# Both feed-forward layers of a decoder trunk by seven block products in place of eight

## The reference, cut to what matters

```python
D_MODEL = 1024; SEQ = 1024; DEPTH = 2; FFN_HIDDEN = 2816      # all float32

def swiglu(h, w_gate, w_up, w_down):
    return (jax.nn.silu(h @ w_gate) * (h @ w_up)) @ w_down

for layer in range(DEPTH):
    h = rmsnorm(x, mix_norm_w[layer])
    x = x + (attn_pool_mixer(h, ...) if layer % 2 == 0 else ssd_mixer(h, ...))
    h = rmsnorm(x, ffn_norm_w[layer])
    x = x + swiglu(h, w_gate[layer], w_up[layer], w_down[layer])
return rmsnorm(x, final_norm_w)
```

## Time and profile before

| what | value |
|---|---|
| median of three runs | 2565.6 us (2565.22 to 2565.96) |
| span of the profiled execution | 2561.2 us |
| PE busy, weight loads busy | 98%, 80% of the span |
| DVE, ACT, POOL busy | 39%, 31%, 25% |
| DMA traffic, mean | 54 GB/s |
| feed-forward of layer 0 | from 326.7 to 1055.2 us |
| feed-forward of layer 1 | from 1834.1 to the end |

### The profile page before, as it was taken

How to read it: one execution, slowest core, us unless ns; L and a number is a source line. 1 busy time by engine, 2 the same in 40 slices (tenths; PEclk the granted TensorE clock), 3 DMA queues, 4 the chain that set the end, 5 groups by cost and what they waited for, 6 DMA issues and landing times.

```text
span 2561.2 us, 30302 instructions
## 1 busy us (share of the span) xinstructions
PE 2507.6 (98%) x11642; PEld 2038.2 (80%) x11642; DVE 1001.9 (39%) x1474; ACT 803.2 (31%) x1311; POOL 627.6 (25%) x340
## 2 busy tenths in 40 slices
PE   7999999999999999999999999999999999999998
PEld 5866788888888888777887887887888888888887
DVE  5345432222222222648438348448522222222224
ACT  4044421111111111448238247248411111111112
POOL 2222222222222222124214214324222222222220
PEclk9999999999999999999999999999999999999999
DMA  4110111111111111112112112212111111111111
GB/s 146 50 33 1 41 60 48 43 46 44 49 49 49 49 49 49 36 58 91 37 59 88 51 49 83 58 51 82 50 58 49 49 49 49 49 49 49 49 33 66
DMA packets 167848, 137.54 MB, mean 54 GB/s; under 512 B 14160, under 2 KB 152284, under 8 KB 167772
## 3 DMA queue, kind: packets, MB, share of 16 engines
q1 hardware_dynamic: 164444, 128.85, 16.7%
q10 hardware_dynamic: 3328, 7.60, 0.8%
HBM read 132.11 MB, written 4.33 MB: 53 GB/s over the span
## 4 chain that ended last, share of the span: by engine, by line
PE 91%; DVE 4%; issue 2%; ACT 2%; POOL 0%; DMA 0%; DVEq 0%; ACTq 0%; POOLq 0%
PE ps L840 28%; PE ps L842 28%; PE ps L841 28%; PE ps L1012 1%; PE ps L980 1%; PE ps L1179 1%; PE ps L873 1%; DVE acc L1514 1%; PE ps L1166 1%; DVE mdec L1553 1%; PE ps L1004 1%; DVE yx L1582 1%; PE ps L1171 1%; DVE xres L1269 1%; DVE xn_lo L1299 1%
## 5 line engine op out<-in xcount | busy, mean ns | idle before, releaser
L840 PE MATMUL ps<-xn_hi,w_hi 128*128 128x512 f32 x2208 | 865.9, 392 | 7.9 <-DVE xn_lo L1299 4.8
L841 PE MATMUL ps<-xn_lo,w_hi 128*128 128x512 f32 x2208 | 860.6, 390 | 0.0
L842 PE MATMUL ps<-xn_hi,w_lo 128*128 128x512 f32 x2208 | 860.1, 390 | 0.0
L474 POOL TENSOR_TENSOR w_lo<-w_raw,w_hi 128x1024 fp32r<-128x1024 f32 x206 | 497.5, 2427 | 1453.8 <-ACT w_hi L564 1453.5
L840 PEld LDWEIGHTS ps<-xn_hi,w_hi 128*128 128x128 f32 x2208 | 415.1, 188 | 100.5 <-issue 12.6
L842 PEld LDWEIGHTS ps<-xn_hi,w_lo 128*128 128x128 f32 x2208 | 415.1, 188 | 87.1
L841 PEld LDWEIGHTS ps<-xn_lo,w_hi 128*128 128x128 f32 x2208 | 415.3, 188 | 84.9
L564 ACT ACTIVATE w_hi<-w_raw 128x1024 fp32r<-128x1024 f32 x206 | 212.5, 1053 | 541.6 <-PE ps L842 357.4
L1434 DVE TENSOR_TENSOR hid<-ps,gate 128x512 f32<-128x512 f32 x88 | 60.9, 692 | 802.4 <-ACT gate L668 802.4
L1269 DVE TENSOR_TENSOR xres<-ps,xres 128x512 f32<-128x512 f32 x368 | 251.2, 690 | 203.8 <-PE ps L842 203.8
L668 ACT ACTIVATE gate<-ps 128x512 f32<-128x512 f32 x88 | 52.6, 598 | 747.0 <-PE ps L842 747.0
(11 more groups left out here) (189 smaller groups left out, 2148.7 us busy)
## 6 DMA issues: line engine op xcount, KB each, us to landing
w_raw<-in_w_gate SPq DMA_DIRECT2D x44, 512.0 KB, 3.8
w_raw<-in_w_up SPq DMA_DIRECT2D x44, 512.0 KB, 4.0
w_raw<-in_w_down SPq DMA_DIRECT2D x44, 512.0 KB, 3.4
w_raw<-in_ssd_w_in SPq DMA_DIRECT2D x40, 512.0 KB, 3.9
mdec<-decay_sums SPq DMA_DIRECT2D x32, 512.0 KB, 3.6
w_raw<-in_ssd_w_out SPq DMA_DIRECT2D x16, 512.0 KB, 4.3
out<-xn ACTq DMA_DIRECT2D x8, 512.0 KB, 2.6
xres<-in_x SPq DMA_DIRECT2D x6, 512.0 KB, 8.4
```

Of the source, the lines that this page charges most:

```text
L474: pool.tensor_tensor(w_lo[piece.slot][:, :], raw[piece.raw][:, :], f(w_hi[piece.slot][:, :]), ALU.subtract).then_inc(lo_done, 1)
L840: pe.matmul(dst, l_hi, r_hi, start=first, stop=False)
L841: pe.matmul(dst, l_hi, r_lo, start=False, stop=False)
L842: return pe.matmul(dst, l_lo, r_hi, start=False, stop=last)
```

## The change

It splits tokens, model width and hidden width in two each, and makes a 2 x 2 by 2 x 2 block product from seven products of sums of blocks (Strassen's scheme in Winograd's form, M1 to M7) in place of eight.

- **Gate and up, stage one.** A pair is 256 hidden columns (`NP` = 11 pairs). A pair has seven products for gate and seven for up. A product is 4 blocks x 3 = 12 matmuls of 512 tokens. M3, M4, M6 and M7 are added by PE on top of a PSUM bank that already holds M5, M7, M1 and M6; before that ACT copies the bank out (`copy_out`). Of the weights, POOL makes four sums per matrix and pair (`w_sum`), ACT seven high parts (`p_hi_of`), POOL seven low parts (`p_lo_of`), each 128 x 512: POOL has 22 such instructions a pair. Gate and up share one set of buffers, so the sum of up can be made only when the same product of gate is done.
- **Token side, once a layer.** The input sums (`comb`, T1 to T4 of the blocks) are made from the last four token tiles as they are transposed: DVE `tail_t1` to `tail_lo2`, ACT `tail_first` to `tail_hi4`, POOL `tail_lo3`, `tail_sum4`, `tail_lo4`. They are written out between the work of pair 0.
- **Hidden layer.** ACT and DVE assemble the four blocks of gate and up, DVE multiplies and makes the sums S1 to S4, and SP stores seven blocks of 128 x 512 a pair to DRAM (`hidden`, 1.8 MB a pair).
- **Down, stage two.** 7 products x 11 pairs = 77 slices of 4 token tiles x 3 = 12 matmuls. SP loads a slice's hidden block and one to two weight blocks (256 KB each) into a ring of five; POOL makes one low part, ACT two high parts, DVE one low part, for 44 slices also a weight sum (`slice_sum`), and between them 56 adds to the residual (`add_down`).
- **Residual.** It is parked in DRAM (`parked_x`) during stage one, as its 32 KB a partition serve as work space, and is loaded again during slices 5 to 19.
- The norms after layer 0 and 1 are placed in the last product of stage two (`plain`, `final`) and behind it. The loops over rounds are written out.

The diff, cut:

```diff
+FIRST_PAIR = ("M1g", "M2g", "M1u", "M2u", "M5g", "M6g", "M3g", "M7g", "M5u", "M4g", "M6u", "M3u", "M7u")
+NEXT_PAIR = ("M2g", "M5g", "M6g", "M3g", "M7g", "M1u", "M4g", "M2u", "M5u", "M6u", "M3u", "M7u")
...
+        hidden = nc.dram_tensor("hidden", (NP, P, 7 * BANK), F32, kind="Internal").ap()
...
+        DOWN = ("M1", "M2", "M5", "M6", "M4", "M7", "M3")
+        ADDS_TO = {"M1": ((4, 0), (4, 1), (0, 0), (0, 1)), "M2": ((4, 0),), "M5": ((4, 1), (0, 1)),
+                   "M6": ((4, 1), (0, 0), (0, 1)), "M4": ((0, 0),), "M7": ((0, 0), (0, 1)), "M3": ((4, 1),)}
...
+                def store_hidden(p):
+                    sp.wait_ge(h_ready, h_order.count(layer, p, "S3"))
+                    sp.dma_start(hidden[p], h_set).then_inc(h_stored, 16)
...
+                sp.wait_ge(out_full, 2 * NT * (1 + layer * G))
+                load_wv("u", 0)
+                for p in range(NP):
+                    if p + 1 < NP:
+                        sp.wait_ge(p_lo_done, lo_order.count(layer, p, "M4g"))
+                        load_wv("g", p + 1)
+                    if p:
+                        store_hidden(p - 1)
+                    sp.wait_ge(p_lo_done, lo_order.count(layer, p, "M4u"))
+                    if p + 1 < NP:
+                        load_wv("u", p + 1)
...
+                def load_slice(j, p):
+                    s, n = j * NP + p, DOWN[j]
+                    i = s % RING
+                    if s in (2, 3):
+                        sp.wait_ge(product_full, product_order.count(layer, NP - 1, "M7u"))
...
+                    elif s >= RING:
+                        sp.wait_ge(down_full, down_count(layer, 0, s - RING))
...
+                    sp.dma_start(s_val[i][:, :], hidden[p][:, j * BANK:(j + 1) * BANK]).then_inc(ring_loaded[i], 16)
...
+                        load_d(d12[p], 0, 1)
+                        load_d(d_val[i][:, :], 0, 0)
...
+                for p in range(4):
+                    load_slice(0, p)
+                store_hidden(NP - 1)
+                back = [4, 0, 5, 1, 6, 2, 7, 3]
+                for s in range(4, SLICES):
+                    load_slice(s // NP, s % NP)
+                    if 5 <= s < 5 + 2 * NT and s % 2:
+                        tt = back[(s - 5) // 2]
+                        sp.wait_ge(parked[tt % 2], 16 * (layer * NT // 2 + tt // 2 + 1))
+                        if s == 5:
+                            sp.wait_ge(h_stored, 16 * (layer + 1) * NP)
...
+                    a, b, op = {5: (a21, a22, ALU.add), 6: (p_val[5][:, :, :], a11, ALU.subtract),
+                                3: (a12, p_val[6][:, :, :], ALU.subtract), 7: (a11, a21, ALU.subtract)}[n]
+                    pool.tensor_tensor(p_val[n][:, :, :], a, b, op).then_inc(sum_ready, 1)
...
+                p_lo_of(0, "M1g")
+                p_lo_of(0, "M2g")
+                tail_lo3(0)
+                tail_sum4(0)
+                w_sum(0, "g", 5)
+                w_sum(0, "g", 6)
+                p_lo_of(0, "M1u")
+                p_lo_of(0, "M5g")
+                p_lo_of(0, "M2u")
+                w_sum(0, "g", 3)
+                p_lo_of(0, "M6g")
+                p_lo_of(0, "M3g")
+                w_sum(0, "g", 7)
+                p_lo_of(0, "M7g")
+                for i in range(1, 4):
+                    tail_lo3(i)
+                tail_lo4(0)
+                for i in range(1, 4):
+                    tail_sum4(i)
+                    tail_lo4(i)
+                p_lo_of(0, "M4g")
+
+                def sums_and_lo(p, m):
+                    w_sum(p, m, 5)
+                    w_sum(p, m, 6)
+                    p_lo_of(p, "M5" + m)
+                    w_sum(p, m, 3)
+                    p_lo_of(p, "M6" + m)
+                    p_lo_of(p, "M3" + m)
+                    w_sum(p, m, 7)
+                    p_lo_of(p, "M7" + m)
+
...
+                for s in range(SLICES):
+                    pool.wait_ge(s_hi_done, layer * SLICES + s + 1)
+                    pool.tensor_tensor(s_lo[s % RING][:, :], s_val[s % RING][:, :], f(s_hi[s % RING][:, :]), ALU.subtract)\
+                        .then_inc(s_lo_done, 1)
...
+                    act.dma_start(parked_x[tt], xres[:, tt, :]).then_inc(parked[tt % 2], 16)
+                    square(tt, ffn_xn(tt))
...
+                copy_out(0, "M1g")
+                tail_hi2(1)
+                tail_hi3(1)
+                tail_hi2(2)
+                tail_hi3(2)
+                p_hi_of(0, "M6g")
+                tail_hi2(3)
+                tail_hi3(3)
+                p_hi_of(0, "M3g")
+                p_hi_of(0, "M7g")
+                copy_out(0, "M1u")
+                for i in range(4):
+                    tail_hi4(i)
+                p_hi_of(0, "M4g")
+
+                copy_out(0, "M5g")
+                p_hi_of(0, "M5u")
...
+                def slice_hi(j, p):
+                    s, n = j * NP + p, DOWN[j]
+                    i = s % RING
+                    act.wait_ge(ring_loaded[i], ring_count(layer, j, p))
...
+                def product(p, mn):
+                    m, n = mn[2], int(mn[1])
+                    pe.wait_ge(p_lo_done, lo_order.count(layer, p, mn))
+                    if p == 0:
+                        if mn == "M1g":
...
+                        elif mn == "M6g":
+                            pe.wait_ge(comb_lo_done, comb_lo_order.count(layer, "T2", 3))
+                        elif mn == "M7g":
+                            pe.wait_ge(comb_pool_done, comb_pool_order.count(layer, "T3lo", 3))
+                        elif mn == "M4g":
+                            pe.wait_ge(comb_pool_done, comb_pool_order.count(layer, "T4lo", 3))
...
+                        pe.wait_ge(t_copied, copy_order.count(layer, p, "M5" + m))
+                    elif n == 7:
+                        pe.wait_ge(t_copied, copy_order.count(layer, p, "M6" + m))
+                    elif n == 4:
+                        pe.wait_ge(c_ready, c_order.count(layer, p, "22" + m))
+                    bank = bank_a(layer, m) if n in (1, 6, 7, 4) else bank_b(layer, m) if n == 2 else bank_c(m)
...
+                    for k in range(H2):
+                        ins = mm3(bank, p_hi[n][:, k, :], p_lo[n][:, k, :], r_hi[:, k, :], r_lo[:, k, :],
+                                  n in (1, 2, 5) and k == 0, k == H2 - 1, n not in (1, 2, 5))
+                    ins.then_inc(product_full, 1)
...
+                def down_slice(j, p):
+                    s = j * NP + p
...
+                    pe.wait_ge(s_lo_done, layer * SLICES + s + 1)
+                    pe.wait_ge(d_lo_done, layer * SLICES + s + 1)
+                    for t_ in range(4):
+                        if p == 0 and j >= 2:
+                            pe.wait_ge(down_added, add_order.count(layer, DOWN[j - 2], t_, *ADDS_TO[DOWN[j - 2]][-1]))
+                        ins = mm3(down_banks(layer, j)[t_], s_hi[i][:, t_ * P:(t_ + 1) * P], s_lo[i][:, t_ * P:(t_ + 1) * P],
+                                  d_hi[i][:, :], d_lo[i][:, :], p == 0, p == NP - 1)
+                        ins.then_inc(down_full, 1)
...
+                pe.wait_ge(pair_freed, t.count("unit"))
+                product(0, "M1g")
+                ffn_T(layer, 6)
+                product(0, "M2g")
+                ffn_T(layer, 7)
+                product(0, "M1u")
+                product(0, "M2u")
+                product(0, "M5g")
+                product(0, "M6g")
+                product(0, "M3g")
+                product(0, "M7g")
+                product(0, "M5u")
+                product(0, "M4g")
+                product(0, "M6u")
+                product(0, "M3u")
+                product(0, "M7u")
...
+                pe.wait_ge(gate_ready, silu_order.count(layer, NP - 1, "21"))
+                pe.wait_ge(c_ready, c_order.count(layer, NP - 1, "12u"))
+                down_slice(0, 0)
+                product(NP - 1, "M4u")
+                for s in range(1, SLICES):
+                    if s == NP:
+                        pe.wait_ge(h_ready, h_order.count(layer, NP - 1, "21"))
+                    down_slice(s // NP, s % NP)
...
+                tail_t1(0)
+                tail_t2(0)
+                tail_t3(0)
+                tail_b22(0)
+                make(6)
+                outs(NT - 1)
+                tail_t4(0)
+                tail_lo1(0)
+                tail_lo2(0)
+                make(7)
+                for i in range(1, 3):
+                    tail_t1(i)
+                    tail_t2(i)
+                    tail_t3(i)
+                    tail_b22(i)
+                    tail_lo1(i)
+                tail_t1(3)
+                tail_t2(3)
...
+                def h_sums(p):
+                    h_block(p, "21")
+                    h_sum(p, "S1", "11", "21", ALU.add, "21")
+                    h_sum(p, "S2", "S1", "12", ALU.subtract, "S1")
+                    h_sum(p, "S4", "22", "S2", ALU.subtract, "S2")
+                    h_sum(p, "S3", "12", "11", ALU.subtract, "S2")
```

(9 more changed lines are left out.)

977 lines of the change are left out of this document (755 added, 222 removed).

## The result

The changed kernel takes 2469.0 us (median of 4 runs, 2467.3 to 2472.5), the kernel before 2565.4 beside it (2562.3 to 2566.0): a ratio of 0.963, 95% interval 0.962 to 0.965. Forecast were 2480, with 2435 to 2540 as the range. The profiled execution's span is 2468.4 us against 2561.2, so 92.8 us went, where the sum of the prediction said 85.2. The rest of the distance to 2480 is the 4.4 us that the forecast put between span and median: here the median is 0.6 above the span, and the profiled execution took 2470.2.

What follows compares the result with a forecast made beforehand. PE's matmuls were taken as the bound (busy 98%). -179.6 + 62.2 + 16 + 8 + 6.4 - 1.3 + 3.1 = -85.2 on the 2561.2 us span gives 2476.0; with 4.4 to the median, 2480, range 2435 to 2540.

Steps and rivals of the forecast that it cites:

- Matmuls: Feed-forward of both layers: 792 fewer matmuls at 0.2268 us each, all on the path, -179.6 us.
- Pairs 1 to 10 cost nothing: Stage one: POOL's cycle, 29.5 + 4.8 = 34.3 us, fits within PE's 38.1 us a pair, so nothing is late.
- the 85% that was to show it: Sign for stage one: POOL's `w_sum` and `p_lo_of` at 1.3 to 1.5 us, with a busy share near 85%.
- The rivals that made POOL the bound: Stage one: 1.82 an instruction gives 2544 us (chance 0.10); at 1.87 the gain is gone (slower, chance 0.05).
- Pair 0: First pair of each layer: 32.5 us of waits, 15.1 at M3 of gate; +62.2 us for both layers.
- Between the stages: Hand-over to stage two: slice 4's load behind the store is 6 us late, +8 a layer, +16 in both.
- The 2 us forecast for `slice_lo(0, 0)`: Between the stages: 2 us of wait for this low part behind DVE's colliding product, within the +8 a layer.
- Stage two: Down slices: DVE's adds and the M5 slices' loads cost +4 us a layer, bounds 0 and 18; +8 in both.
- the rival's 248 GB/s: Stage two bound by its loads at this rate: up to 18 us a layer, 2508 us, chance 0.08.
- The exclusive lock: POOL and DVE excluding each other for whole instructions: stage two would lose 5 to 10 us more a layer; not adopted.
- Clock: Lower granted clock behind the waits for M3 and slice 4: 4 x 1.6 = +6.4 us, bounds 0 and 15.
- Ends: After layer 0's feed-forward -1.3 us; after layer 1's last matmul, adds, squares, norms and store, +3.1 us.

Runs made afterwards that it cites:

- 7/8 run: The kernel before with one eighth of the feed-forward matmuls (792) left out and nothing else changed: 2391.8 us, ratio 0.933.
- the run with fewer matmuls: The changed kernel without the third matmul (weights' low part) in three of four blocks, pairs 1 to 10 of gate/up: 2360.6 us.
- the run with only the copies first: The changed kernel with ACT's copies of M5g's and M6g's banks in pair 0 ahead of four T4 high parts and M4g's: 2471.0 us, ratio 0.963.

## Why the prediction was right, point by point

**Matmuls.** The count and the price held. The 7/8 run puts 173 of 179.6 us on them alone, and in the changed kernel they start every 0.227 us from pair 1 on.

**Pairs 1 to 10 cost nothing.** Right: 38.08 us a pair, 38.1 forecast. The instruction was put at 1.34 and is 1.36 on average (290 us in 213 instructions of stage one in layer 0), but that already holds the collisions: 29.9 us a pair. Adding 4.8 us for seven of them was too much; the run with fewer matmuls gives 32.6 where the prediction said 34.3. So POOL is busy 77% here and not the 85% that was to show it. It did not matter with 38.1 to go. The rivals that made POOL the bound (1.82 or 1.87 an instruction) are refuted: the strided form is no dearer than the flat one.

**Pair 0.** The mechanism was right, M3 of gate on ACT's `copy_out`, twice; the sizes were too large: 11.4 us and not 15.1, and 23.6 in place of 32.5 over all waits, for the seventh tile 1.9 (2.3), M1 of up 3.7 (4.4), M2 0.6 (2.6), M5 0.8 (1.5), M6 5.2 (5.3), M7 0 (1.3). The error of M3 lies in where its chain starts. ACT came to M6's high part at 347.54, which is 24.0 us behind the start of the transposes, and not at 27.1. From there to the end of the copy it took 22.2 us, close to the 22.6 between the prediction's 27.1 and 49.7, but by luck: the prediction's own terms (17.4, 3 and 3.9) come to 24.3, so the copy would have ended at 51.4. Of the 3 us for collisions 1.4 came (three instructions of POOL's up to 353.3 take 1.70 and not 1.22); from 355 us on DVE is idle and there are none. ACT and POOL then hand over every 3.22 us:

```profile
347.54 0.62 ACT L991 ACTIVATE p_hi<-p_val 128x512 fp32r<-128x512 f32 x1
...
363.44 1.26 POOL L758 TENSOR_TENSOR t_val<-t_val,xn_lo 128x512 f32<-128x512 f32 x1
...
364.74 0.63 ACT L1032 ACTIVATE t_hi<-t_val 128x512 fp32r<-128x512 f32 x1 [2.59 <-POOL t_val L758]
...
365.44 1.26 POOL L765 TENSOR_TENSOR t_lo<-t_val,t_hi 128x512 fp32r<-128x512 f32 x1 [0.74 <-ACT t_hi L1032]
```

What the prediction did not see is that this wait had two causes of one size. POOL's queue of the tail makes the copy late, as it said, but it makes the low part of M5 of up late as well, two products on. Moving the copy won nothing, moving POOL's work won 21.7 us in all.

**Between the stages.** 19.6 against 19.2 with the clock: right in size and cause. The load of slice 4 stands 0.4 us behind the 1792 KB store, and the store takes 6.7 us to land. The 2 us forecast for `slice_lo(0, 0)` were 0.2 to 0.6 (ahead of slice 3).

**Stage two.** +0.5 in place of +8, the largest error in proportion. The loads keep up, and the rival's 248 GB/s was no ceiling. Between 800 and 820 us the DMA moved 331 GB/s, loads of 256 KB and reloads of 512 KB together. In the slices of M5, whose loads are all of 256 KB and are the densest, it moved 274 and PE never waited:

```profile
850.00:870.00 20.00, 20.00 (x89) 16.10 (x88) 14.98 (x19) 9.42 (x15) 12.08 (x8) 1.00 0.82 274
```

The Trainium skill (DMA: Bandwidth & Descriptors, Bandwidth) gives 138 GB/s for a transfer of 64 KB and 341 for one of 1 MB. The trace's 274 with loads of 256 KB lies between them; it is what these slices asked for, so how much more such loads could move is not shown.

**The exclusive lock.** The trace agrees with the rule that the prediction didn't trust: two engines that take turns at 1.7 us, against 0.60 + 1.22 alone. The Trainium skill (SBUF: State Buffer, Who interferes with whom) says that DVE, when it reads two SBUF operands, and POOL, when it reads SBUF, exclude each other for a whole instruction. The 5 to 10 us a layer that the prediction derived from it for stage two came from the term 2 x 0.69. Successive DVE instructions start 0.60 us apart, 0.69 is the length with the overlap of the next. So a slice with a sum is 1.22 + 2 x 0.60 = 2.4 us of locked time, an estimate from these starts, and fits into 2.72.

**Clock.** +6.4 was forecast as 4 x 1.6, behind M3's and slice 4's waits alone. The waits of M1 of up (3.6 us) and M6 (5.0) bring the lower clock too: the first pairs paid 5.5 and 5.9 us and slice 4 1.9 and 1.7, together 15.0. This term was less than half of what came.

In a stage that the change doesn't touch, the state-space part, 5.1 us more are lost by the same 3809 matmuls. They lie behind pauses of 2.5 to 2.6 us ahead of the product with `mdec`, of which this stage has four in every run. Here is what follows the second one: in the changed kernel, in the kernel before, and in the run with only the copies first, whose instructions in this stage are those of the changed kernel.

```profile
1347.30:1350.50 3.20, 2.83 (x18) 2.41 (x19) 2.13 (x4) 0.81 (x2) 2.52 (x1) 0.50 0.50 142
```

```profile
1398.50:1401.70 3.20, 3.20 (x26) 2.64 (x25) 3.10 (x8) 2.24 (x4) 2.41 (x2) 1.00 0.36 107
```

```profile
1348.10:1351.30 3.20, 3.20 (x26) 2.62 (x27) 2.98 (x8) 2.15 (x4) 2.41 (x2) 1.00 0.37 110
```

And PE's pause ahead of it, in the changed kernel and with the copies first:

```profile
1347.67 1.55 PE L1778 MATMUL ps<-mdec,xdt 128*64 128x128 f32 x12 [2.57 <-DVE mdec L2377]
```

```profile
1348.01 1.09 PE L1778 MATMUL ps<-mdec,xdt 128*64 128x128 f32 x16 [2.54 <-DVE mdec L2377]
```

From one such pause to the next it is 187.7 us at the full clock and 189.3 with a stretch of 0.50 behind the pause. In the changed kernel's profile the clock fell behind all four pauses, in the profile of before and in that of copies first behind one. Three times 1.6 to 1.7 is the 5.1. So these 5 us are no price of the change: the same instructions behind the same pauses had them in one execution and not in another. Why the clock falls behind one pause of this length and not behind the next, no run here shows.

**Ends.** After layer 1 the prediction had 3.1 and it is 5.5. It missed that ACT writes its last four stores behind all four squares, so they are issued in a row at the very end:

```profile
2461.47 2.90 ACTq L1189 DMA_DIRECT2D out<-xres  x4
...
2461.99 1.28 DVE L1881 SCALAR_TENSOR_TENSOR xres<-xres,small,norm_wp 128x1024 f32<-128x1024 f32 x1
```

That leaves 5.1 us from the end of the last norm (2463.3) to the end, 3.1 before. After layer 0 `dt_rows(1)` waited 2.7 (3.1 forecast), and the first tile's transposes 1.9, which were not in the sum.

In all: pair 0 was forecast 9 too dear (its waits 17 too dear, its clock 8 too cheap) and stage two 7.5, and the state-space part (5.1) and the ends (4.7) were missing. The mechanisms held, all but the clock's size; that the total is right within 8 us is partly luck, because these errors offset each other. The forecast's own bounds add up to 2538 at the top and not to 2530; the range given holds both.

## What to carry to other kernels

A wait names its last releaser, not all that were late: before you move the named instruction, ask when the next operand would have been ready, and expect nothing if the answer is "at the same time". In an in-order stream, put an instruction where its own operand is done, for a wait there holds up everything behind it; and put a large store where nobody behind it on the queue is needed within its own duration. Work moved from POOL to an idle DVE is free only as far as POOL idles at that moment.

## What the runs showed of the hardware

- DVE with two SBUF operands and POOL, 128x512 each: 0.68 and 1.25 us alone, 1.74 and 1.73 side by side, so nearly nothing of it runs at the same time. Holding POOL back for 2 us made DVE's chain 2.1 us shorter.
- Four 256 KB loads issued 0.4 to 3.1 us behind a store of 1792 KB on the same queue landed 6.5 to 7.7 us after their issue, in both layers; the medians of such loads over the program are 2.8 to 3.8.
- The granted clock fell to 0.50 behind pauses of 3.6, 5.0, 7.6 and 11.2 us and not behind the seventh tile's 1.8 and 2.0. Behind pauses of 2.5 to 2.6 us it fell in some executions and not in others, at 1.6 to 1.7 us each.
- GpSimd reads the strided four-block form at the price of the flat one: 1.28 us for 128x512 (`p_val<-wv_u` with nobody beside it), against 1.30.
